# Decoder trunk on one core: four value groups of a layer as two pairs of seven block products

## The reference

```python
hn = rmsnorm(x, g_mix)
proj = hn @ w_in                     # 512 x 1024 times 1024 x 9728
qa, ka, va, qr, kr, vr, gr, ga, gb = jnp.split(proj, SPLIT_POINTS, axis=-1)
# va: attention values, 1536 columns: three groups of 512, dilation 1, 4, 16
# vr: retention values, 1024 columns: four heads of 256
```

## Time and profile before

| | us |
|---|---|
| median of 3 runs | 1881.01 (1880.67 to 1881.52) |
| profiled execution, its time | 1880.63 |
| its span in the trace | 1878.8 |
| PE busy | 1863.8 (99%) |
| DVE busy | 1255.0 (67%) |
| ACT busy | 837.6 (45%) |
| SP's queue, share of 16 DMA engines | 33.8% (201.03 MB) |
| POOL's queue, share of 16 DMA engines | 10.6% (33.56 MB) |

### The profile page before, as it was taken

The page is one execution under the profiler, slowest core; times in us unless marked ns, Lnnn a source line. Parts: engine busy times, 40 slices in busy tenths (PEclk is TensorE's granted clock), DMA queues, the critical chain, the costliest instruction groups (busy, mean ns, idle before and its releaser), DMA issues.

```text
span 1878.8 us, 22972 instructions
## 1 busy us (share of the span) xinstructions
PE 1863.8 (99%) x9064; PEld 1548.6 (82%) x9064; DVE 1255.0 (67%) x1848; ACT 837.6 (45%) x1234; POOL 129.0 (7%) x104
## 2 busy tenths in 40 slices
PE   9999999999999999999999999999999999999998
PEld 8888888887888888888788888888878888888886
DVE  5356778767447576776863568788674575667777
ACT  7325465464224344434472254554642233434445
POOL 0001111100000000000000112112000000000010
PEclk9999999999999999999999999999999999999999
DMA  4544233333333465557626333243243334655675
GB/s 147 202 157 121 82 90 113 89 98 90 129 97 123 124 145 133 139 139 202 150 86 241 95 109 104 74 121 105 68 145 99 105 113 112 135 149 142 135 210 126
DMA packets 210668, 236.93 MB, mean 126 GB/s; under 512 B 13569, under 2 KB 160769, under 8 KB 209537
## 3 DMA queue, kind: packets, MB, share of 16 engines
q1 hardware_dynamic: 192944, 201.03, 33.8%
q0 software_dynamic: 16896, 33.56, 10.6%
q10 hardware_dynamic: 720, 0.87, 0.1%
HBM read 219.57 MB, written 13.77 MB: 124 GB/s over the span
## 4 chain that ended last, share of the span: by engine, by line
PE 91%; DVE 4%; ACT 2%; DMA 2%; issue 1%; POOL 0%; DVEq 0%; ACTq 0%; POOLq 0%
PE pj L1853 20%; PE pj L1855 20%; PE pj L1854 20%; PE sc L2159 2%; PE sc L2161 2%; PE yr L2161 2%; PE yr L2159 2%; PE sc L2163 2%; PE yr L2163 2%; PE pt L2159 1%; DMA w_raw<-in_w_down 1%; PE pt L2161 1%; PE pt L2163 1%; DVE w_lo L1178 1%; PE yr L1960 1%; PE pt L1961 1%
## 5 line engine op out<-in xcount | busy, mean ns | idle before, releaser
L1853 PE MATMUL pj<-h_hi,w_hi 128*128 128x512 f32 x1408 | 554.4, 394 | 1.0 <-DVE sA L1553 1.0
L1855 PE MATMUL pj<-h_hi,w_lo 128*128 128x512 f32 x1408 | 548.5, 390 | 0.0
L1854 PE MATMUL pj<-h_lo,w_hi 128*128 128x512 f32 x1408 | 548.3, 389 | 0.0
L1178 DVE TENSOR_TENSOR w_lo<-w_raw,w_hi 128x1024 fp32r<-128x1024 f32 x283 | 334.9, 1220 | 129.0 <-ACT w_hi L707 127.8
L707 ACT CAST w_hi<-w_raw 128x1024 fp32r<-128x1024 f32 x280 | 282.9, 1050 | 291.8 <-PE pj L1855 56.9
L1853 PEld LDWEIGHTS pj<-h_hi,w_hi 128*128 128x128 f32 x1408 | 264.3, 188 | 59.1 <-issue 1.9
L1855 PEld LDWEIGHTS pj<-h_hi,w_lo 128*128 128x128 f32 x1408 | 264.2, 188 | 56.0
L1854 PEld LDWEIGHTS pj<-h_lo,w_hi 128*128 128x128 f32 x1408 | 264.4, 188 | 53.8 <-issue 0.5
L1132 POOL TENSOR_TENSOR rcos<-rot,tables 128x512 f32<-128x512 f32 x64 | 87.2, 1363 | 693.7 <-ACT rot L833 634.7
L1000 ACT ACTIVATE relu<-pj 128x512 f32<-128x512 f32 x64 | 38.2, 597 | 185.2 <-PE pj L1855 185.2
L722 ACT CAST w_hi<-gh 128x1024 fp32r<-128x1024 f32 x80 | 79.9, 1050 | 82.0 <-PE yr L2163 30.5
(11 more groups left out here) (340 smaller groups left out, 3134.9 us busy)
## 6 DMA issues: line engine op xcount, KB each, us to landing
w_raw<-in_w_in SPq DMA_DIRECT2D x151, 512.0 KB, 4.7
w_raw<-in_w_up SPq DMA_DIRECT2D x64, 512.0 KB, 4.7
gh<-in_w_down POOLq DMA_DIRECT2D x26, 1024.0 KB, 8.7
gh<-in_w_down SPq DMA_DIRECT2D x16, 1024.0 KB, 5.8
w_raw<-in_w_down SPq DMA_DIRECT2D x20, 512.0 KB, 5.0
w_raw<-in_w_b SPq DMA_DIRECT2D x16, 512.0 KB, 3.5
w_raw<-in_w_o SPq DMA_DIRECT2D x16, 512.0 KB, 3.9
u<-in_w_down POOLq DMA_DIRECT2D x6, 1024.0 KB, 13.2
```

The source lines that it names most:

```text
L1178: nc.vector.tensor_tensor(w_lo[s][:, c], src[:, c], w_hi[s][:, c], ALU.subtract).then_inc(lo_done, 1)
L1853: nc.tensor.matmul(out, w_hi[s][:, wc], acts[0], start=first, stop=False)
L1854: nc.tensor.matmul(out, w_hi[s][:, wc], acts[1], start=False, stop=False)
L1855: return nc.tensor.matmul(out, w_lo[s][:, wc], acts[0], start=False, stop=last)
```

## The change

In each layer group 0 of the values stays as it is. The other four groups become two pairs: the two retention groups (q = 0) and the attention groups 1 and 2 (q = 1). A pair is a product of a 2 x 2 block matrix of activations (token half x k half) by a 2 x 2 block matrix of weights (k half x group). It is computed by seven block products, called 1, 5, 2, 6, 3, 7, 4 in their order. A product is one unit of 1 MB of weights with 4 k tiles x 2 token blocks x 3 = 24 matmuls.

- The weights of products 1, 2 and 3 are plain blocks through `w_raw`. Those of 5, 6, 7 and 4 are sums, made in three SBUF slots (`gh[0]`, `gh[1]`, `v_slot`): SP loads or copies 1 MB, POOL's queue adds 1 MB. Eight such additions per layer.
- The activations of 5, 6, 3 and 7 are sums too: DVE adds or subtracts 128 x 1024 of `h32`, ACT makes the high part, DVE the low part. In the second pair the sum is made by four strided DVE instructions.
- `h32` keeps the scaled `x` in float32 for all 8 tiles. The copies `res_hi`/`res_lo` go: in the second pair, products 1, 2 and 4 read `h_hi`/`h_lo` as stationary operand with a stride of four elements.
- Banks are read out in steps: ACT writes the first share to `vA` (`value_read`, behind products 1, 5, 6, 4), DVE adds the second (`value_finish`, behind 2, 3, 7).
- Retention values stay float32 in DRAM and come back as one DMA (`vR`); the split into high and low is made per head in the pair stage.
- `x_out` (the spill) and the fetch of `rstd` in residue order move ahead of most of the value stage's loads on SP's queue.

The diff, cut to its core:

```diff
+    V_ORDER = (1, 5, 2, 6, 3, 7, 4)
...
+    V_PAIRS = (COL_VR // 512, 2 * GROUPS + 1)
+    V_SLOT = {(0, 5): 0, (0, 7): 0, (0, 6): 1, (0, 4): 1, (1, 5): 2, (1, 6): 0, (1, 4): 0, (1, 7): 1}
...
+                    to = v_slots[slot][:]
+                    if i == 6:
+                        first = V_SLOT[q, 5]
+                        sp.wait_ge(v_added[first], (l * V_ADDS[first] + V_ADD[q, 5]) * 16)
+                        sp.dma_start(to, v_slots[first][:]).then_inc(v_in[slot], 16)
...
+                def vR_away(part, m, b0):
+                    if part < 3:
+                        sp.wait_ge(v_out, last_read(l, 0, (2, 3, 7)[part]))
+                    else:
+                        sp.wait_ge(v_first, first_read(l, 0, 4))
+                    to = vr_scratch[:, 2 * m:2 * m + 2].rearrange("p h (b c) -> p b h c", b=TB)
+                    src = vA[:, b0:b0 + 2, AW + m * 512:AW + m * 512 + 512].rearrange("p b (h c) -> p b h c", h=2)
+                    for b in range(2):
+                        sp.dma_start(to[:, b0 + b], src[:, b]).then_inc(vr_sent[part], 16)
...
+                value_weights()
+                if l > 0:
+                    sp.wait_ge(lo_done, m_unit(l - 1, "D", CH - 1, 3) * 2 + 2 + UNIT_CREDIT)
+                value_slot(0, 5)
+                value_raw(0, 1)
+                x_out()
+                value_slot(0, 6)
+                if l > 0:
+                    sp.wait_ge(a_ready, l * LD)
+                value_slot(1, 5)
+                value_raw(0, 2)
                 residues_of_rstd()
-                value_weights(2)
-                vR_away(0)
-                value_weights(3)
-                vR_away(1)
-                value_weights(4)
-                x_out()
+                value_slot(0, 7, (0, 5))
+                value_raw(0, 3)
+                vR_away(0, 0, 0)
+                value_raw(1, 1)
+                value_slot(1, 6, (0, 7))
...
+                value_slot(1, 7, (0, 4))
+                vR_away(2, 1, 2)
+                value_raw(1, 2)
+                vR_away(3, 0, 2)
                 sp.wait_ge(rot_out, l * 8 * PAIRS + 1)
                 sp.dma_start(tables[:], a["tables"]).then_inc(tables_in, 16)
+                value_raw(1, 3)
...
-                nc.scalar.copy(res_hi[:, k, :].rearrange("p (r m) -> p r m", r=4), by_residue(h_hi[:, k, :]))
-                nc.scalar.copy(res_lo[:, k, :].rearrange("p (r m) -> p r m", r=4),
-                               by_residue(h_lo[:, k, :])).then_inc(res_done, 1)
+                nc.scalar.copy(h_hi[:, k, :], normed(J, k, k)).then_inc(h_hi_done, 1)
...
+                def set_high(q, i):
+                    p = V_SUMS.index((q, i))
+                    if p >= SETS:
+                        act.wait_ge(mm_done, v_unit(l, *V_SUMS[p - SETS]) * 2 + 2 + MM_CREDIT)
+                    act.wait_ge(v_sum, l * 8 + p + 1)
+                    nc.scalar.copy(a_sets[(p + 1) % SETS][0][:], ssum_v[p % 2]).then_inc(v_set_hi, 1)
+
+                def value_read(q, i):
+                    act.wait_ge(mm_done, v_unit(l, q, i) * 2 + 2 + MM_CREDIT)
+                    act.wait_ge(nrstd_done, 2 * l + 1 + q)
+                    if q == 1:
+                        act.wait_ge(vr_sent[{1: 0, 6: 1, 5: 2, 4: 3}[i]], (l + 1) * 32)
+                    m, b0 = {1: (0, 0), 5: (1, 2), 6: (1, 0), 4: (0, 2)}[i]
+                    by = nrstd if i == 5 else rstd
+                    for b in range(2):
+                        nc.scalar.activation(vA[:, b0 + b, AW + m * 512:AW + m * 512 + 512],
+                                             vbank(l, q, i)[:, b * S:(b + 1) * S], ACT.Copy,
+                                             scale=by[:, q * TB + b0 + b:q * TB + b0 + b + 1]).then_inc(v_first, 1)
+
...
+                        pool.wait_ge(lo_done, v_unit(l, q, 6) * 2 + 2 + UNIT_CREDIT)
+                    else:
+                        pool.wait_ge(v_in[slot], (l * V_INS[slot] + V_IN[q, i]) * 16)
...
+                    nc.gpsimd.dma_start(v_slots[slot][:].rearrange("p (k c) -> p k c", k=4),
+                                        w_in_v[l, :, 4 * h:4 * h + 4, V_PAIRS[q] + m, :],
+                                        accum_op=ALU.add).then_inc(v_added[slot], 16)
+
+                for q, i in ((0, 5), (0, 6), (1, 5), (0, 7), (0, 4), (1, 6), (1, 7), (1, 4)):
+                    add_values(q, i)
...
+                    if i in (6, 3):
+                        dve.wait_ge(v_sum, l * 8 + p)
+                    x0, x1, op = {5: (a21, a22, ALU.subtract), 6: (to[0], a11, ALU.subtract),
+                                  3: (to[1], a12, ALU.add), 7: (a11, a21, ALU.subtract)}[i]
...
+                        mm = nc.vector.tensor_tensor(to[p % 2][:, k], x0[:, k], x1[:, k], op)
...
+                    m, b0 = {2: (0, 0), 3: (1, 0), 7: (1, 2)}[i]
+                    by, op = nrstd if i == 7 else rstd, ALU.add if i == 2 else ALU.subtract
+                    dve.wait_ge(mm_done, v_unit(l, q, i) * 2 + 2 + MM_CREDIT)
+                    dve.wait_ge(v_first, first_read(l, q, {2: 1, 3: 6, 7: 5}[i]))
+                    for b in range(2):
+                        to, r = vA[:, b0 + b, AW + m * 512:AW + m * 512 + 512], q * TB + b0 + b
+                        nc.vector.scalar_tensor_tensor(out=to, in0=vbank(l, q, i)[:, b * S:(b + 1) * S],
+                                                       scalar=by[:, r:r + 1], in1=to, op0=ALU.mult,
+                                                       op1=op).then_inc(v_out, 1)
...
+                value_low(V_U)
+                value_sum(0, 5)
+                set_low(0, 5)
+                value_sum(0, 6)
+                for s in range(2 * VN):
+                    q, pos = s // VN, s % VN
+                    before = ((s - 1) // VN, V_ORDER[(s - 1) % VN])
+                    if s > 0 and before[1] in (2, 3, 7):
+                        value_finish(*before)
+                    value_low(V_U + s + 1)
...
+                    if s == 4:
+                        rms_spread(l)
+                    if pos == 1:
+                        set_low(q, 3)
+                        value_sum(q, 7)
+                    if pos == 2:
+                        set_low(q, 7)
+                    if s == 4:
+                        value_sum(1, 5)
+                    if s == 5:
+                        dve.wait_ge(rstd_res, l * 16 + 16)
+                        negated(TB)
+                        set_low(1, 5)
+                        value_sum(1, 6)
+                    if s == 6:
+                        set_low(1, 6)
+                        value_sum(1, 3)
...
+                    nc.vector.tensor_tensor(vR_lo[:], vR[:, 0:TB - 1, :], vR_hi[:], ALU.subtract).then_inc(vr_lo, 1)
...
+                    kt, half = {1: (k, 0), 2: (k + 4, 0), 4: (k + 4, 1)}[i]
+                    return v[:, kt, (2 * half + b) * P:(2 * half + b + 1) * P] if q == 0 else \
+                        by_residue(v[:, kt, :])[:, 2 * half + b]
...
+                    elif i == 4:
+                        pe.wait_ge(v_out, last_read(l, q, 7))
...
+                        if k % 2 == 0:
+                            weights(n, k // 2)
...
+                            if i in (1, 2, 4):
+                                hi, lo = (value_operand(q, i, v, k, b) for v in h)
+                            else:
+                                hi, lo = (v[:, k, b * P:(b + 1) * P] for v in a_sets[(V_SUMS.index((q, i)) + 1) % SETS])
+                            out = vbank(l, q, i)[:, b * S:(b + 1) * S]
+                            nc.tensor.matmul(out, hi, w_hi[n % 2][:, w], start=opens and k == 0, stop=False,
...
+                for q in range(2):
+                    for i in V_ORDER:
+                        if (q, i) == (0, 3):
+                            spread(l)
+                        value_product(q, i)
+                pe.wait_ge(rstd_all_done, 2 * l + 1)
```

365 lines of the change are left out of this document (214 added, 151 removed).

## The result

The changed kernel takes 1915.07 us (median of 4 runs, 1913.89 to 1916.11), the kernel before 1881.26 in the same comparison: a ratio of 1.0177 with a 95% interval of 1.016 to 1.0195. The forecast was 1902 with a range of 1875 to 1912. The sign was right, the size was not: 34 us slower and not 21, 3 us beyond the range.

The account below looks back on a forecast made before the run. PE bounds the kernel: 21.8 us of matmuls saved, but stalls on transfers in the value stages outweigh them, leaving stages 10.6 and 11.6 us longer. +22 us on 1880.6 gives 1903 profiled, 1902 forecast; range 1875 to 1912.

Parts of the forecast that it names:

- What bounds the kernel: Whole kernel: PE, busy 1863.8 of 1878.8 us; a matmul removed is a gain, a wait a loss, one for one.
- part 1: Value stages: 48 fewer matmuls per layer at 0.2267 us, 10.9 us per layer, 21.8 saved in all.
- The sum of the stalls: Value stages behind group 0: late transfers make PE wait, stages 10.6 and 11.6 us longer, +22 us; waits about 50.
- T: Start of the value stage behind group 0 in a layer; 963.1 us in the second layer before the change.
- The step that failed: From first pair's product 4 to stage end: eight products at 5.44 us each, 43.5 us, plus 1.7 for a read-out.
- The cause given for the stalls: First pair: SP's wait on the rstd write delays slot 7's load, then additions 7 and 4; product 4 at T+53.4.
- Part 3: Pair stage: extra cast and low part per head, about 0.9 us each, hidden in idle gaps; cost 0, uncovered 7 us.
- Part 4: Second pair's products 1, 2, 4: strided stationary loads cost 0, with 12 us kept for the range.
- (a): Faster rival: transfers keep up, only DVE's order (4.2 us late at product 4) and read-outs hold PE; 1874 us, chance 0.15.
- (b): Rival: rstd write blocks SP, but additions and loads do not slow each other; product 4 at T+43.5, 1884 us, chance 0.12.
- (c): Rival: the change doesn't cost anything; 1859 to 1868 us, chance 0.04.
- (d): Rival: strided loads cost as well, the forecast plus up to 12 us, to 1914; chance 0.13.

Follow-up runs that it names:

- the old order: Changed kernel without its 16 additions of 1 MB to slots, queues and lists left as they were: 1884.99 us.
- its last move: Against the kernel with queues and lists in order of need (1903.01 us), spill of x put behind the following stage's second weight load: 1887.53 us.
- the run with both moves: Changed kernel with the read of rstd_scratch behind product 3's weights and the spill of x behind the last retention values: 1903.44 us.

## Why the prediction was wrong

**What bounds the kernel, and part 1.** Right. PE hardly stood idle before (8.3 us of waits), and 96 matmuls went at the price of a row.

**The sum of the stalls.** Right in size, though not in each place. PE's waits were to grow to about 50 us and are 48.6, and the DMA share was 0.92 to 1.06 from T-5 to T+60. In the second layer product 7 ran from T+41.2 (forecast T+40.6), additions 7 and 4 landed at T+38.7 and T+47.4 (T+38.3 and T+45.1), DVE's list took 8.1 us (8.3). The write of `rstd` landed sooner than forecast (T+16.0, not T+21) and slot 7's load took 12.9 us and not 5.8, so that two errors met at slot 7: T+29.2, forecast T+27.3. The addition for 7 then took 9.2 us and not 11, which hid this by luck. The forecast had the copy for product 6 landed at T+3.5 and product 2 two to four us late; product 2 was 0.4 us late, and product 6, whose addition took 15.7 us, waited 6.5. Product 4 started at T+55.6 instead of T+53.4. In the first layer it was T+58.7: the write of `rstd` went out at T+8.3, since ACT reached the square root only behind product 5's conversion, and the 1.0 us allowed for this layer was too little. Product 5 there, put at up to 2.7 us late, waited 4.1.

**The step that failed** is "Product 4 and the seven of the second pair take 8 x 5.44 = 43.5". The first of them runs behind a wait of 7 us at half clock. From product 4's start to the end of the stage it was 49.05 and 48.96 us, less 1.7 for the last read-out 47.4 and 47.3: 3.9 and 3.8 more than the term, 3.0 and 2.9 of it the clock and 0.6 in each the stride. That makes 7.7 of the 13.5 us by which the stages (107.8 and 104.5) exceed the forecast's 100.2 and 98.6; the other 5.8 are product 4's later start. With the 22.2 of the forecast this is the 35.7 measured. Without the clock's 5.9 the measured time would be about 1909, inside the range, and the run with unread matmuls in that wait took 1909.8. The clock was in no row of the kernel before: its longest wait of PE was 1.6 us. Its price could not be read there, but a stall of 7 us in a kernel that had none should have put a bound on it: half clock over one product, up to 5.4 us per layer. The Trainium skill (TensorE: Matmul & The Clock Gate, HAM oscillation) describes products that start at the lower clock because each came behind a wait for a transfer, and here the trace agrees (0.50 behind 7.1 us of idling). The prediction drew on another page and passed over this one.

**The cause given for the stalls** was half wrong. "SP stands at the wait on it, as it did before, but what is queued behind it now is due much sooner" is true and costs 2 to 3 us in all, not ten per layer as its removal was expected to bring. What rows 7 say, that additions and loads slow each other, is the better account (393 GB/s is the row of plain transfers, 198, the last one, that of additions alone, 259 that of both): moving the read of `rstd` changed the order and kept the bytes, moving the spill took bytes away, and only the second moved product 4 by what it should. The Trainium skill (DMA: Bandwidth & Descriptors, Queues, rings and completion order) says that each DMA engine takes packets in turn from the queues that have work; slot 7's load, issued 13 us earlier and 7 us slower, fits that.

**Part 3** held: no wait of PE in the pair stages points to `value_split`. **Part 4** took 0 for the stride and measured 1.2 us; the 12 kept for the range were far off. Of what the prediction took from the Trainium skill (SBUF — State Buffer, on SBUF cachelines), "for free" is refuted by the 0.235; that each crossing to a new line pays agrees with it.

**The rivals.** (a) at 1874 left out the clock; even with no additions at all the old order gives 1885. Its 9.6 us of work on DVE come to 8.7 by the forecast's own figures, so that its 4.2 lies near the measured 4.0 partly by luck. (b) and (c) did not occur; in (b), T+34 plus the 8.3 of DVE's list is T+42.3 and not T+43.5. (d) would have ended at 1914, and 1915 was measured, but with a tenth of its mechanism: the number was near for a wrong reason.

## What to carry to other kernels

A trade of matmuls for transfers has to be costed twice: in the matmul's time and in whether the DMA engines have that many bytes to spare just there. When they are full, an earlier issue gives little of its lead to the landing, and what helps is to move bytes that nobody waits for out of the stretch (here one spill of 2 MB, 15 us between the medians at its last move, about half of that between the profiled runs). Of stalls, count the clock too, but only where no later wait takes it over.

## What the runs showed of the hardware

PE's granted clock falls to its lower level while PE stands idle (0.50 behind 7.1 us), and the product behind it pays: 2.9 to 3.0 us more after 7 us and 1.9 after 6.5. The price does not grow steadily with the wait: when the same kernel ran again it was 2.7 us after 7.4 and 2.4 after 8.5. Waits of 2.5 us cost 0.1 once (product 6, first layer) and 1.6 another time (product 7, second layer); after the 2.0 us that fillers had left it was 0.2. A 128 x 512 matmul whose stationary operand takes every fourth float32 follows the one before by 0.235 us instead of 0.2267. An accumulating transfer of 1 MB took 8.3 us to land with little beside it (in the run with both moves) and up to 23.8 with others under way (in the run with the read moved); a 1 MB load beside them up to 19.5 us where 5.8 was the median before. With additions under way the engines showed a share of 1.08 at 200 GB/s from 991 to 1011 us in the changed kernel: full, at half of what plain transfers move.
